# Delta net in a hybrid diffusion layer: pairwise decays from broadcast rows of cumulated log gates on ScalarE and VectorE instead of matmuls with triangular masks

## What is computed

```
gcum = jnp.cumsum(to_chunks(g[..., None])[..., 0], axis=-1)
decay = jnp.exp(jnp.where(causal, gcum[..., :, None] - gcum[..., None, :], -jnp.inf))
m = jnp.where(strict, jnp.einsum('nbhid,nbhjd->nbhij', k_beta, kc) * decay, 0.0)
sol = lax.linalg.triangular_solve(eye + m, rhs, left_side=True, lower=True, unit_diagonal=True)
attn = jnp.einsum('nbhid,nbhjd->nbhij', qc, kc) * decay
...
v_new = u_i - jnp.einsum('bhck,bhkv->bhcv', w_i, S)
o = jnp.einsum('bhck,bhkv->bhcv', q_i, S) + jnp.einsum('bhij,bhjv->bhiv', attn_i, v_new)
S = S * jnp.exp(gl)[..., None, None] + jnp.einsum('bhck,bhcv->bhkv', k_i, v_new)
```

## Time and profile before

| | |
|---|---|
| median of 3 runs | 1324.57 us (1323.89 to 1327.45) |
| the profiled execution, its time | 1325.24 us |
| the profiled execution, its span | 1323.4 us |
| granted PE clock, mean | 0.994 of full speed |
| PE busy | 1292.8 us, 98% |
| DVE, ACT, POOL busy | 65%, 51%, 21% |
| the eight steps | about 338 to 534 us from the span's start |

### The profile page before, as it was taken

The page is one execution under the profiler, slowest core; times in us unless marked ns, Lnnn a source line. Parts: engine busy times, 40 slices in busy tenths (PEclk is TensorE's granted clock), DMA queues, the critical chain, the costliest instruction groups (busy, mean ns, idle before and its releaser), DMA issues.

```text
span 1323.4 us, 27167 instructions
## 1 busy us (share of the span) xinstructions
PE 1292.8 (98%) x10915; PEld 1219.2 (92%) x10915; DVE 857.9 (65%) x1271; ACT 673.0 (51%) x1087; POOL 283.1 (21%) x360
## 2 busy tenths in 40 slices
PE   6999999999899999999999999999999999999998
PEld 3899899999798898999999999999999988999998
DVE  3764798996666675532777555666737666866663
ACT  4458888867545544313533211332236665664553
POOL 3000132422777886421000000000220001100002
PEclk8999999999999999999999999999999999999999
DMA  9632233225423112124466565555324221557662
GB/s 324 196 102 81 80 84 93 81 81 197 155 81 112 65 49 87 59 97 138 157 191 191 190 192 191 186 195 177 114 94 138 87 65 38 181 179 216 190 200 81
DMA packets 141308, 179.11 MB, mean 135 GB/s; under 512 B 11296, under 2 KB 122208, under 8 KB 140944
## 3 DMA queue, kind: packets, MB, share of 16 engines
q1 hardware_dynamic: 137312, 168.94, 40.6%
q10 hardware_dynamic: 3280, 8.46, 1.8%
q0 software_dynamic: 608, 0.19, 0.1%
HBM read 176.44 MB, written 1.11 MB: 134 GB/s over the span
## 4 chain that ended last, share of the span: by engine, by line
PE 77%; DVE 11%; ACT 5%; POOL 3%; issue 3%; DMA 1%; SPq 0%; DVEq 0%; ACTq 0%; POOLq 0%
PE bank L2770 55%; PE bank L2778 4%; DVE w_lo L1807 3%; DVE qkv L1893 2%; PE bank L3169 2%; PE bank L3178 2%; ACT w_hi L963 1%; PE bank L2696 1%; POOL qkv L821 1%; PE bank L3441 1%; PE bank L3464 1%; DMA first_w<-in_w_mod 1%; PE bank L3048 1%; PE bank L3107 1%; PE bank L3123 1%
## 5 line engine op out<-in xcount | busy, mean ns | idle before, releaser
L1807 DVE TENSOR_TENSOR w_lo<-raw,w_hi 128x1024 fp32r<-128x1024 f32 x212 | 265.5, 1253 | 297.6 <-ACT w_hi L963 297.4
L963 ACT ACTIVATE w_hi<-raw 128x1024 fp32r<-128x1024 f32 x212 | 223.5, 1056 | 378.2 <-PE bank L2770 376.4
L2770 PE MATMUL bank<-h_hi,w_hi 128*128 128x256 f32 x1472 | 298.4, 281 | 5.9 <-DVE w_lo L1807 3.4
L2770 PE MATMUL bank<-h_hi,w_lo 128*128 128x256 f32 x1472 | 293.6, 278 | 0.0
L2770 PE MATMUL bank<-h_lo,w_hi 128*128 128x256 f32 x1472 | 288.4, 278 | 0.0
L2770 PEld LDWEIGHTS bank<-h_hi,w_hi 128*128 128x128 f32 x1472 | 225.4, 188 | 14.7 <-issue 9.5
L2770 PEld LDWEIGHTS bank<-h_hi,w_lo 128*128 128x128 f32 x1472 | 225.3, 188 | 0.0
L2770 PEld LDWEIGHTS bank<-h_lo,w_hi 128*128 128x128 f32 x1472 | 222.4, 188 | 0.6 <-DVE h_lo L2107 0.4
L2770 PE MATMUL bank<-hid_hi,w_hi 128*128 128x256 f32 x768 | 171.9, 278 | 0.0
L2770 PE MATMUL bank<-hid_lo,w_hi 128*128 128x256 f32 x768 | 170.8, 277 | 0.0
L2770 PE MATMUL bank<-hid_hi,w_lo 128*128 128x256 f32 x768 | 170.7, 277 | 0.0
(11 more groups left out here) (381 smaller groups left out, 2401.7 us busy)
## 6 DMA issues: line engine op xcount, KB each, us to landing
raw<-in_mlp_w SPq DMA_DIRECT2D x128, 512.0 KB, 3.7
late_w<-in_w_mod SPq DMA_DIRECT2D x56, 512.0 KB, 4.4
raw<-in_even_w_in SPq DMA_DIRECT2D x48, 512.0 KB, 3.8
raw<-in_w_mod SPq DMA_DIRECT2D x24, 512.0 KB, 4.5
first_w<-in_w_mod SPq DMA_DIRECT2D x16, 512.0 KB, 11.1
raw<-in_even_w_out SPq DMA_DIRECT2D x16, 512.0 KB, 3.7
raw<-in_attn_w_qkv SPq DMA_DIRECT2D x16, 512.0 KB, 3.6
d_qd<-eg_rows ACTq DMA_DIRECT2D x16, 256.0 KB, 4.2
```

What stands on the lines that cost most here:

```text
L963: act.activation(stored(w_hi, j, four), raw[:, j % RAW], ACT.Copy).then_inc(hi_ready, 1)
L1807: dve.tensor_tensor(stored(w_lo, j, four), raw[:, j % RAW], stored(w_hi, j, four).bitcast(F32), ALU.subtract).then_inc(split_done, 1)
L2770: return pe.matmul(bank[2 * pair + t][:, c - n0:c - n0 + CTX], w_[:, k, t * P:(t + 1) * P], x_[:, c:c + CTX], start=(kk == 0 and first and ...
```

## The change

The four matmuls, the four POOL multiplications and the split of the gates are gone. ACT now writes three tables `g_tok` from the bank of cumulated gates: their exponentials, the sums themselves and their negatives (12 small instructions instead of 4). PE transposes the first two at once (128 rows), four units of matmuls earlier than before; ACT copies them and writes them to DRAM, now ahead of `l2_load(0)`. For each step ACT loads eight rows of sums broadcast into `d_lg` (512 KB, `gate_rows`), double-buffered. In it ACT adds the negated sum of each partition's own token to the four tiles of one direction (`forward_gates`), DVE subtracts the own sum in the other four and takes the smaller of both (`log_decay`), and ACT takes the exponential from SBUF (`decay`). The two broadcast loads of `d_qd` become one.

```diff
+            def rows_out():
+                act.wait_ge(s_gps, 4)
+                act.activation(eg_row[:, :], bank[X1][:, 0:P], ACT.Copy).then_inc(s_gate, 1)
+                act.wait_ge(s_gate, 7)
+                act.dma_start(eg_dram[:, :], eg_row[:, :]).then_inc(s_egw, 16)
...
+            def forward_gates(q):
+                act.wait_ge(s_rows_in[q % 2], rows_landed(q))
+                for i in range(4):
+                    r_ = 8 * q + 4 + i
+                    y_ = d_lg[q % 2][:, 1, i]
+                    ins = act.activation(y_, y_, ACT.Identity, bias=g_tok[:, NEG_LG, r_:r_ + 1])
+                alink(ins)
+                shifted[q] = acount[0]
             def decay(q):
-                act.wait_ge(p_dc, q + 1)
+                act.wait_ge(v_lg, q + 1)
                 if q >= 2:
                     act.wait_ge(g_at, 2 * q - 2)
-                act.activation(flat(d_dt[q % 2][:, :, :]), bank[R0 if q else R2][:, :], ACT.Exp).then_inc(a_dt, 1)
+                act.activation(flat(d_dt[q % 2][:, :, :]), flat(d_lg[q % 2][:, 0]), ACT.Exp).then_inc(a_dt, 1)
...
                 flipped(q, LAST, 0)
+                if q + 2 < STEPS:
+                    forward_gates(q + 2)
                 tokens(q, 0)
...
+            def log_decay(q):
+                dve.wait_ge(link_a, shifted[q])
+                dve.wait_ge(s_rows_in[q % 2], rows_landed(q))
+                for i in range(4):
+                    r_ = 8 * q + i
+                    y_ = d_lg[q % 2][:, 0, i]
+                    ins = dve.scalar_tensor_tensor(out=y_, in0=y_, scalar=g_tok[:, LG, r_:r_ + 1], in1=d_lg[q % 2][:, 1, i],
+                                                   op0=ALU.subtract, op1=ALU.min)
+                ins.then_inc(v_lg, 1)
...
                 reduced(q, 3, 1)
+                if q + 2 < STEPS:
+                    log_decay(q + 2)
...
-                for d in range(2):
-                    for g_ in (d_gu, d_gl):
-                        mm = pe.matmul(bank[R0 if q else R2][:, :], lines[:, d], flat(g_[:, d]),
-                                       start=(d == 0 and g_ is d_gu), stop=(d == 1 and g_ is d_gl))
-                mm.then_inc(p_dc, 1)
-            def k_k(q):
-                pe.wait_ge(a_dt, q + 1)
```

More of the change, by code:

```diff
@@ L433, in build @@
         solved = [0] * 8
+        shifted = [0] * 8
         dcount = [0]
@@ L1212, in body_beside @@
                     if b == LRU_TILES:
+                        decay(0)
                         l2_rstd(2)
@@ L1384, in beside @@
                             x_ = eg_[:, 2 * cp:2 * cp + 2, d, :] if d else eg_[:, 2 * cp:2 * cp + 2, d, :][:, ::-1, :]
-                            y_ = eg_tok[:, :].rearrange("p (g e c a) -> p g e c a", e=4, c=2, a=2)[:, :, 2 * cp + d]
-                            act.activation(y_, x_.rearrange("p c (g a) -> p g c a", a=2), ACT.Exp)
+                            for k_, f_, by_ in ((EG, ACT.Exp, 1.0), (LG, ACT.Copy, 1.0), (NEG_LG, ACT.Copy, -1.0)):
+                                y_ = g_tok[:, k_].rearrange("p (g e c a) -> p g e c a", e=4, c=2, a=2)[:, :, 2 * cp + d]
+                                act.activation(y_, x_.rearrange("p c (g a) -> p g c a", a=2), f_, scale=by_)
                     for buf, c_ in ((neg_eg, 0), (e_rest, 64)):
@@ L1389, in beside @@
                     ins.then_inc(s_gate, 1)
+                if b == LRU_TILES and w == 2:
+                    gate_rows(0)
+                    gate_rows(1)
                 if b == LRU_TILES and w == 3:
@@ L1392, in beside @@
                     l2_rstd(1)
-                    act.wait_ge(s_gps, 4)
-                    act.activation(eg_row[0:8 * STEPS, :], bank[X0][0:8 * STEPS, 0:P], ACT.Copy).then_inc(s_gate, 1)
-                    act.wait_ge(s_gate, 7)
-                    act.dma_start(eg_dram[:, :], eg_row[0:8 * STEPS, :]).then_inc(s_egw, 16)
+                    forward_gates(0)
                     betas(0)
-                    decay(0)
                     l2_load(1)
@@ L2045, in body_beside @@
                     spread(0)
+                    log_decay(1)
                 beside(b, 2)
@@ L2052, in body_beside @@
                 if b < LRU_TILES + 1:
+                    if b == LRU_TILES:
+                        log_decay(0)
                     split_lo(u + 5, 5)
@@ L3049, in four, with k_k @@
                 return mm
-            def decay(q):
-                pe.wait_ge(g_gu, 2 * q + 2)
-                if q >= 2:
+            def k_k(q):
+                if q == 0:
+                    pe.wait_ge(s_gate, 6)
+                elif q >= 2:
                     pe.wait_ge(a_tok, 2 * q - 2)
-                elif q == 0:
-                    pe.wait_ge(g_gate, 2)
-                for d in range(2):
-                    for g_ in (d_gu, d_gl):
-                        mm = pe.matmul(bank[R0 if q else R2][:, :], lines[:, d], flat(g_[:, d]),
-                                       start=(d == 0 and g_ is d_gu), stop=(d == 1 and g_ is d_gl))
-                mm.then_inc(p_dc, 1)
-            def k_k(q):
-                pe.wait_ge(a_dt, q + 1)
                 four(R0 if q else R2, lambda i: feat(8, q, i), lambda i: feat(8, q, i)).then_inc(p_kk, 1)
@@ L3278, in _ @@
                 mod_filler(mods_in(q, 0))
-                if prep:
-                    decay(q + 1)
                 if tail:
```

77 lines of the change are left out of this document (32 added, 45 removed).

## The result

The changed kernel takes 1332.36 us (median of 12 runs, 1329.94 to 1335.36), the kernel before in the same session 1325.03 (12 runs, 1322.64 to 1328.86): 7.3 us more, a ratio of 1.0048 with a 95% interval of 1.0038 to 1.0059. I had said 1326.0, at most 1330.5. The direction of the sum was right, its size wrong, and the time lies outside the range.

The account below looks back on a forecast made before the run. PE, busy for 98% of the span, was taken as the bound. Lost 1.5 us (z segment) - 0.5 (step 0) - 0.2 (seam 0) + 0.6 (seams 1 to 5) = 1.4, on 1324.57: 1326.0 us, range 1320 to 1330.5.

Parts of the forecast that it names:

- What is removed: Eight steps: 7.4 us of PE's matmuls, some PE waits and POOL's 16 multiplications go; the latter give nothing more alone.
- Step 0: I count 0.5 us gained: Step 0: the exponential no longer waits 0.62 us for PE, counted as 0.5 us gained; its matmuls give nothing.
- The z segment: Ahead of step 0: ACT's additions (1.1 us) and the first `log_decay` (0.4) lengthen the chain, 1.5 us lost.
- the late `l_four`: z segment: this load comes 1 to 2 us late, using up the 0.93 us of step 0's matmuls and no more.
- Seams 0 to 5: Between steps: seam 0 gains 0.2 us, seams 1 to 5 together lose 0.6 us.
- PE's matmuls alone would give 4.6: Seams 1 to 5: 4.6 us gained from PE's matmuls alone, against the 0.6 us lost that was forecast.
- first rival: Seams 1 to 5: DVE isn't held up by POOL's masks, 4.6 us gained there, 1320.4 us in all; chance 0.24.
- second rival: z segment: `l_four` lands 3 us later still and shifts the chain up to step 0, 1329.2 us; chance 0.24.

Follow-up runs that it names:

- e1: Changed kernel with POOL's two removed splits of the gates put back, unread, ahead of its first multiplication by the sigmoid; 1329.81 us, ratio 1.0033.
- e7: Kernel before with its two splits of the gates on POOL moved behind POOL's 18 multiplications by the sigmoid; 1328.52 us, ratio 1.0026.
- e14: e5 with one wait more: POOL's multiplication of the betas for step 1 starts only after DVE's last scaling of the keys; 1322.82 us, ratio 0.9974.
- e5: Changed kernel with the edits of e1, e2 and e3 together; 1323.72 us, ratio 0.9982 to the kernel before.
- e12: Changed kernel with POOL's splits back and the additions and subtractions of steps 0 and 1 left out (decays wrong); 1326.35 us, ratio 1.0017.
- e4: Changed kernel with one wait more: POOL's two masks of a seam start only after DVE's four subtractions there; 1329.56 us, ratio 1.0029.
- e11: Kernel before with three of the four decay matmuls of every step left out (decays wrong); 1324.30 us, ratio 0.9997.
- e3: Changed kernel with the additions and subtractions of the six later steps moved from the seams into the middle of the step; 1327.66 us, ratio 1.0014.
- e2: Changed kernel with ACT's additions and DVE's subtractions for step 1 put elsewhere in the z segment, where each idled; 1329.66 us, ratio 1.0043.

## Why the prediction was wrong

- **"What is removed"** failed first. I listed the matmuls and POOL's large multiplications (32 in the trace, not the 16 that I wrote), wrote nothing of the rest, and gave the sum no term ahead of the z segment. Two removed splits of 1.17 us each on an engine with nothing to do cost 2.2 us (e1, e7), since they had kept POOL's next work away from DVE's. I knew the rule that the two hold each other up and used it for the seams only.
- **"Step 0: I count 0.5 us gained"** had the wrong sign: 2.1 us were lost, all of them from the second product to the neighbours of step 1, which took 12.41 us in place of 10.25. An exponential that no longer waits 0.62 us for PE is a POOL multiplication that starts earlier, beside DVE's scalings: 0.8 us (10.55 in e14 against 11.34 in e5). TensorE's clock, which I had nowhere, is most of the rest: PE idled 2.53 us for the turned block instead of 0.97, and the clock then stood at the lower level for some 3 us. In the ten traces with a wait of 2.51 or 2.53 us there, the clock fell within 1.6 us of its end in eight (not in e5 and e14); in the six with 0.97 to 1.77 us it never did. I have no run that parts the clock alone; its size is from pairs of traces. The part took 12.41 us in the changed kernel and 11.34 in e5, with the same collision, the same 2.5 us of wait ahead of it and no fall: 1.1 us. And with e5 and e14, the same code but for the wait, the part from the neighbours of step 1 to those of step 2 took 22.37 us at full clock and 24.02 with a fall, with the same waits of PE. About 0.3 us of the 2.1 stays without a cause.
- **The z segment** (+1.5) came out at +1.7, but by luck. Up to the fourth sum of squares 0.9 us were gained (62.62 in place of 63.54), since the late `l_four` did not use up step 0's matmuls as I had said: it was issued 3.4 us later but landed within 4.9 us of its issue in place of 7.8. From there to the second product 2.6 us were lost (19.08 in place of 16.50), where I had 1.5: 0.9 up to the first product, which I had as unmoved, and 1.6 behind it. ACT's list was the chain, as I said, but ACT also idled 1.88 us for DVE's late scaling, and DVE's four took 2.20 us beside POOL's `spread`, of which I had hidden most. Without the sixteen instructions (e12) 0.7 of the 2.6 us are left.
- **Seams 0 to 5** were right: +0.4 - 0.55 measured, +0.6 - 0.2 forecast. ACT's four took 1.26 to 1.28 us where I took 1.35. The Trainium skill (ScalarE: Activation LUTs, Rules for kernel authors), by which I had made an estimate of 1.63 us, gives in its section What ACT_TABLE_LOAD costs also an overlap of some 93 ns between neighbours; with it the estimate would have been 1.27, and the trace agrees.
- DVE's four took 2.88 us beside the masks and 1.14 without (e4). The Trainium skill (SBUF - State Buffer, SBUF: two separate sides) says that whichever of VectorE and GpSimd starts first keeps the shared pair of ports for its whole instruction. By that a new start time on POOL is a new price on DVE, and the traces of gates, step 0 and seams agree (2.36 against 1.22 us, 3.42 against 2.35, 2.88 against 1.14).
- **"PE's matmuls alone would give 4.6"** is wrong. Three of four taken out gave 0.9 us over the steps (e11), and all four with POOL's multiplications gone and nothing in the seams 2.9 to 3.5 (e3, e5). So my first rival was priced wrong too: with DVE's four not held up (e4) the steps gain 1.9 us on the kernel before, not 4.6.
- The 0.8 us behind seam 5 (PE waits 0.72 us for the neighbours of step 7) I had not seen at all; the step with it is 1.2 to 1.4 us shorter in e3 and e4.
- The second rival (the late load) had the right sign by luck: the load cost nothing, the loss lay elsewhere. What the range lacked was a case for work that comes earlier than before on POOL.

The same collision accounts for those 0.8 us, and for the steps of e1 and e12, which take 0.9 us more than in the changed kernel (all of it in one step, 26.5 against 25.6, where PE waits 0.71 us for the neighbours in e1). DVE's last multiplication for the neighbours takes 0.42 us when it starts just ahead of POOL's subtraction for `head_lo` (changed kernel at 451.70), and 1.4 us when it starts just behind it (changed kernel at 501.39, e1 at 451.11). Timeline of the changed kernel, DVE and POOL:

```profile
451.70 0.42 DVE L2345 TENSOR_TENSOR d_b<-vec 128x256 f32<-128x256 f32 x1
451.84 1.41 POOL L886 TENSOR_TENSOR head_lo<-qkv,mix_hi 128x512 fp32r<-128x512 f32 x1
...
501.25 1.27 POOL L886 TENSOR_TENSOR head_lo<-qkv,mix_hi 128x512 fp32r<-128x512 f32 x1
501.39 1.41 DVE L2345 TENSOR_TENSOR d_b<-vec 128x256 f32<-128x256 f32 x1
```

No run holds the two apart there, so this rests on the rows alone. Left open is what chooses the pace of the last stretch.

## What to carry to other kernels

Removing work from an engine that no one waits for is not free: list what stands behind it in its queue, when that starts now, and what runs beside it on the engine that it shares with. Where two engines hold each other up, a wait that keeps them apart can be worth more than the work one saves: one wait on POOL gave 2.9 us in the steps (e4), less up to 0.8 lost in step 0, and another gave 0.8 in a part of step 0 (e14), too little for the medians to show. New work belongs where its engine idles and the other is in short instructions, not where its input happens to be ready.

## What the runs showed of the hardware

The same stream of matmuls ran at one of two paces, at full granted clock both times. All matmuls of one line between 1200 and 1300, in the kernel before and in the changed one (duration in ns, minimum, median, maximum):

```profile
L2770 PE MATMUL bank<-hid_hi,w_lo x167: 276/276/277, 1199.8 to 1299.8; 128*128 128x256 f32 x167
```

```profile
L2795 PE MATMUL bank<-hid_hi,w_lo x156: 281/281/281, 1199.7 to 1299.7; 128*128 128x256 f32 x156
```

From 1240 to 1290 PE issued 443 against 427 matmuls, 113 against 117 ns from start to start, which makes 208 or 213 us of the last stretch in all sixteen traces, nothing between. The four traces of the kernel before and its variants all had 208, of the twelve of the changed one and its variants seven had 213. In e2 the twelve times lie in two groups, eight from 1327.9 to 1329.9 and four from 1334.8 to 1335.8; the profiled one, with 213, is in the second. A difference of 0.3% in this kernel can be read from a trace by stretches, and hardly from medians.

The clock fell behind idle times of PE that are short: 2.53 us with 0.8 us of work in 3 us ahead of it in the changed kernel, in e7 behind a wait of 1.89 us that the kernel before had too, without a fall. In e5 and e14 the same wait of 2.5 us brought none.
